# Matmul order in the FFN up projections of a two-layer trunk: both column halves of a strip per input block, high parts first and then low parts

## The reference

```python
D_MODEL = 1024
SEQ = 256
DEPTH = 2
FFN_HIDDEN = ((8 * D_MODEL + 3 * 256 - 1) // (3 * 256)) * 256      # 2816
...
    for i in range(DEPTH):
        ...
        mix = jnp.concatenate([prim, mo], axis=-1) @ w_out[i]
        h = h + rmsnorm(mix, post_mix_g[i])
        hn = rmsnorm(h, pre_ffn_g[i])
        gu = hn @ w_ffn_in[i]
        ff = (jax.nn.silu(gu[..., :FFN_HIDDEN]) * gu[..., FFN_HIDDEN:]) @ w_ffn_out[i]
        h = h + rmsnorm(ff, post_ffn_g[i])
    return h
```

## Time and profile before

| | |
|---|---|
| median of 3 runs | 777.34 us (775.53 to 777.49) |
| the profiled execution, its own time | 776.1 us |
| its span in the trace | 774.4 us |
| PE busy | 745.0 us, 96% of the span |
| DVE, ACT, POOL busy | 446.5, 393.7, 106.5 us |
| 640 matmuls of 512 columns in the wide strips (L1026) | 226.5 us busy |
| 640 matmuls of 256 columns in the wide strips (L1028) | 179.7 us busy |

### The profile page before, as it was taken

How to read it: one execution, slowest core, us unless ns; L and a number is a source line. 1 busy time by engine, 2 the same in 40 slices (tenths; PEclk the granted TensorE clock), 3 DMA queues, 4 the chain that set the end, 5 groups by cost and what they waited for, 6 DMA issues and landing times.

```text
span 774.4 us, 15179 instructions
## 1 busy us (share of the span) xinstructions
PE 745.0 (96%) x6549; PEld 639.3 (83%) x6549; DVE 446.5 (58%) x645; ACT 393.7 (51%) x654; POOL 106.5 (14%) x163
## 2 busy tenths in 40 slices
PE   5999999999999999999999999999899999999996
PEld 4789966678888888888888878999788888888885
DVE  4777886647766566432242638533657756756423
ACT  5835766548645455422465435523248545555311
POOL 8020076500000000000300056500000000000000
PEclk9999989999999999999999999999999999999999
DMA  9847700026655555464733330000055655655411
GB/s 311 301 142 234 251 31 2 2 84 222 203 170 194 187 174 207 166 209 154 237 112 115 120 136 20 4 5 4 3 168 187 195 186 178 202 167 206 172 54 55
DMA packets 78277, 111.71 MB, mean 144 GB/s; under 512 B 2124, under 2 KB 64738, under 8 KB 78210
## 3 DMA queue, kind: packets, MB, share of 16 engines
q1 hardware_dynamic: 77090, 107.67, 41.9%
q0 software_dynamic: 976, 3.04, 1.2%
q10 hardware_dynamic: 144, 0.04, 0.0%
HBM read 109.68 MB, written 1.05 MB: 143 GB/s over the span
## 4 chain that ended last, share of the span: by engine, by line
PE 89%; DVE 5%; ACT 3%; issue 1%; DMA 1%; POOL 0%; DVEq 0%; SPq 0%; ACTq 0%
PE ps L1026 19%; PE ps L726 11%; PE ps L1187 10%; PE ps L727 10%; PE ps L728 10%; PE ps L1028 10%; PE ps L1014 8%; PE ps L760 2%; PE ps L895 1%; PE ps L869 1%; PE ps L846 1%; DMA hn<-mem 1%; DVE row_max L1896 1%; ACT scores L1411 1%; DVE x_hi_lo L2046 1%
## 5 line engine op out<-in xcount | busy, mean ns | idle before, releaser
L1825 DVE TENSOR_TENSOR w_lo<-w_raw,w_hi 128x2048 fp32r<-128x2048 f32 (+2 forms) x90 | 202.2, 2260 | 83.7 <-ACT w_hi L1359 83.6
L1026 PE MATMUL ps<-x_hi_lo,w_hi 128*128 128x512 f32 x640 | 226.5, 399 | 0.0
L1359 ACT ACTIVATE w_hi<-w_raw 128x2048 fp32r<-128x2048 f32 (+2 forms) x90 | 168.0, 1886 | 38.9 <-PE ps L728 37.6
L1028 PE MATMUL ps<-x_hi_lo,w_lo 128*128 128x256 f32 x640 | 179.7, 281 | 0.0
L1026 PEld LDWEIGHTS ps<-x_hi_lo,w_hi 128*128 128x128 f32 x640 | 120.3, 188 | 29.8
L1028 PEld LDWEIGHTS ps<-x_hi_lo,w_lo 128*128 128x128 f32 x640 | 120.9, 189 | 0.0
L726 PE MATMUL ps<-w_hi,x_hi_lo 128*128 128x512 f32 (+3 forms) x208 | 74.1, 356 | 2.8 <-DVE x_hi_lo L2046 2.0
L727 PE MATMUL ps<-w_lo,x_hi_lo 128*128 128x512 f32 (+3 forms) x208 | 72.2, 347 | 0.0
L728 PE MATMUL ps<-w_hi,x_hi_lo 128*128 128x512 f32 (+3 forms) x208 | 72.1, 347 | 0.0
L726 PE MATMUL ps<-w_hi,hidden_hi 128*128 128x512 f32 x176 | 69.6, 395 | 0.0
L728 PE MATMUL ps<-w_hi,hidden_lo 128*128 128x512 f32 x176 | 69.5, 395 | 0.0
(11 more groups left out here) (365 smaller groups left out, 1012.5 us busy)
## 6 DMA issues: line engine op xcount, KB each, us to landing
w_raw<-w_ffn_in SPq DMA_DIRECT2D x44, 1024.0 KB, 5.0
w_raw<-w_ffn_out SPq DMA_DIRECT2D x22, 1024.0 KB, 5.0
w_raw<-rwkv_w_in SPq DMA_DIRECT2D x11, 1024.0 KB, 5.4
w_raw<-w_out SPq DMA_DIRECT2D x8, 1024.0 KB, 5.0
w_raw<-nsa_w_in SPq DMA_DIRECT2D x6, 1024.0 KB, 15.0
w_raw<-w_mem_kv SPq DMA_DIRECT2D x2, 1024.0 KB, 8.9
w_raw<-nsa_cmp_k_w SPq DMA_DIRECT2D x2, 1024.0 KB, 5.5
w_raw<-nsa_cmp_v_w SPq DMA_DIRECT2D x2, 1024.0 KB, 5.4
```

The lines of the kernel that those rows point to most:

```text
L1026: pe.matmul(psum[:, bank + j, :], kt_of(w_hi, i, k)[:, c], xx[:, k, :, :].rearrange("p c n -> p (c n)"), start=k == 0, stop=False)
L1028: ins = pe.matmul(psum[:, bank + j, 0:SEQ], kt_of(w_lo, i, k)[:, c], xh[:, k, :], start=False, stop=k == KD - 1)
L1359: act.activation(w_hi[:, i % SPL, 0:size(i)], raw[:, i % RAW, 0:size(i)], ACT.Copy).then_inc(hi_done, 1)
L1825: dve.tensor_tensor(w_lo[:, i % RAW, 0:size(i)], raw[:, i % RAW, 0:size(i)], w_hi[:, i % SPL, 0:size(i)], ALU.subtract).then_inc(lo_done, 1)
```

## The change

Inside `wide_strip` the loops change places. Before, half 0 went through all 8 input blocks, high and low matmul in turn, and then half 1. Now each input block is gone through once: the 512-column matmul of half 0, that of half 1, then the 256-column matmul of half 0, that of half 1. The operands, the sizes, the number of matmuls and of weight loads, the waits and the increment of `used` are the same.

```diff
             def wide_strip(i, bank):
 
                 pe.wait_ge(lo_done, split_no(i) + 1)
-                for j in range(2):
-                    c = slice(P * j, P * j + P)
-                    for k in range(KD):
-                        pe.matmul(psum[:, bank + j, :], kt_of(w_hi, i, k)[:, c], xx[:, k, :, :].rearrange("p c n -> p (c n)"),
+                cols = [slice(P * j, P * j + P) for j in range(2)]
+                for k in range(KD):
+                    for j in range(2):
+                        pe.matmul(psum[:, bank + j, :], kt_of(w_hi, i, k)[:, cols[j]], xx[:, k, :, :].rearrange("p c n -> p (c n)"),
                                   start=k == 0, stop=False)
-                        ins = pe.matmul(psum[:, bank + j, 0:SEQ], kt_of(w_lo, i, k)[:, c], xh[:, k, :],
+                    for j in range(2):
+                        ins = pe.matmul(psum[:, bank + j, 0:SEQ], kt_of(w_lo, i, k)[:, cols[j]], xh[:, k, :],
                                         start=False, stop=k == KD - 1)
                 ins.then_inc(used, 1)
```

## The result

The changed kernel takes 771.85 us (median of 4 runs, 770.31 to 773.02) beside 777.41 us for the kernel before in the same measurement (4 runs). The ratio is 0.9939, 95% interval 0.9918 to 0.996: it is faster, by 3.1 to 6.4 us. The forecast was no change, with 770.9 to 781.6 as the range and 16 in 100 for faster. Ratios leave out one of e4's ten runs, which took 1058.93 us at a mean granted clock of 0.656, where its other nine had 0.993 to 0.996; what lowered the clock there is not known.

The account below looks back on a forecast made before the run. The prediction took PE's own pace to bound the wide strips. Every term came to 0 us, leaving the profiled execution's 776.1 us, put at 777.3 to suit the runs' median; range 770.9 to 781.6.

Parts of the forecast that it names:

- rival 2: Wide strips: spare time between matmuls shrinks in the new order, −6.4 us to 770.9, or −4.3 us to 773.0; 16 in 100.
- What bounds the kernel: Wide strips: nothing but PE's own pace sets them; PE is busy for 745.0 of 774.4 us.
- Count of work, waits, consumers, weight loads: Wide strips: equal instruction counts, no added waits, consumers and slots released as before, loads hidden under matmuls; 0 us each.
- Rival 1: Second narrow slot of each group: a weight load shows, +22.4 us, or +2.3 to +4.3 in small form; 13 in 100.
- PSUM banks: Wide strips: changing bank costs nothing, and writing the second bank 2.8 us earlier adds no wait; 0 us.
- Rival 3: Wide strips: changing banks with every matmul makes PE wait and lowers its clock, +226.1 us to 1003; 1 in 100.
- Order of the matmuls: Groups of four in wide strips: spacings summed from other loops give 0.7067 us, as before the change; 0 us.

Follow-up runs that it names:

- e4: Changed kernel's order of widths and banks, but half 1 takes the input block beside half 0's, so no neighbours share a block; ratio 0.9963 to the kernel before.
- e2: Kernel before with widths still alternating, but 512-column matmuls of one half interleaved with 256-column ones of the other, changing bank behind nearly every matmul; ratio 1.0.
- e5: Kernel before with all 16 wide matmuls of a strip first, halves by turns, then the 16 narrow ones; ratio 0.9962.
- e3: Kernel before, still half 0 then half 1, but two input blocks at a time as 512, 512, 256, 256 to one bank; ratio 0.9956.
- e1: Kernel before with each input block gone through once, but widths alternating: 512 and 256 of half 0, then of half 1; ratio 1.0007.
- e10: Kernel before with the hidden tiles and the small tiles behind them moved up by 256 bytes in each partition; 777.15 us in one run.
- e12: Kernel before with input tile `x_hi_lo` and all that stands behind it moved up by 384 bytes in each partition, weights unmoved; ratio 0.9956.
- e9: Kernel before with the hidden tiles and the small tiles behind them moved up by 640 bytes in each partition; ratio 0.996.
- e7: Kernel before with only the last wide strip of each layer ordered 512, 512, 256, 256 to one bank; 774.8 us in one run.
- e8: Kernel before with one more PE wait ahead of each layer's down projection, until ACT has copied the last strip's results; ratio 1.0021.

## Why the prediction was wrong in its mechanism, and right in its range

The forecast was "same within 0.3%", and that did not come: the kernel is faster by more. The time of 771.85 us lies in the range all the same, 0.95 us above its lower end. That end was priced for rival 2, from the lowest spacings of two other loops, and neither loop's spacings are what the strips took; that it held is partly luck.

**What bounds the kernel.** Right. PE is busy for all of each stretch before and after, the clock stands at 1.00 in both, and PE waits for nobody in the strips.

**Count of work, waits, consumers, weight loads.** Right, at 0 us each. Loads in the second narrow slot are hidden; narrow pairs even got shorter. Rival 1 did not occur.

**PSUM banks.** Right at 0: e2 changes the bank behind nearly every matmul and keeps 5.653 us, ratio 1.0. Rival 3 did not occur: the granted clock is 1.00 in the strips of the changed kernel and of e2. The Trainium skill (TensorE: Matmul & The Clock Gate, A second HAM failure mode: psum-queue depth-cycling) tells of a kernel that cycles through PSUM banks, idles briefly between groups of matmuls and swings between the two clocks. These two traces change banks and show no such swing.

**Order of the matmuls.** This step failed: "a matmul's cost here goes by its own width and not by its neighbour's". I had priced the new order from pure runs, 2 × 0.2333 + 2 × 0.120 = 0.7067 us, and took it as proof that this was what the alternating group cost. It was a coincidence: two errors cancelled. In the alternating strips a wide matmul costs 0.2367 us, 0.0033 more than priced, and a narrow one 0.1167, 0.0033 less; the earlier trace rows already had 0.24 and 0.11 to 0.12 as single spacings. The 0.2333 was the down projection's own value at its own place in memory, and a run of 16 wide ones in the strips has 0.228 (e5). Nor are the mixed orders sums of pure ones: pairs cost 0.6967, alternation 0.7067. It is rival 2 that came, at half its price: 0.010 us a group in place of 0.0201, 3.2 us in place of 6.4. "Nothing in the trace ties it to the order" was true of that trace, and I read it as evidence against, though the out and the down projection with equal shapes and unequal spacings said plainly that my price list lacked a variable.

**What the cause is, and what stays open.** Shown: the change's gain comes with grouping equal widths. e3 has the grouping without the other two, e1 and e2 have the other two without it, and every trace with grouped widths has strips of 5.57 to 5.59 us in both layers. Alternating strips have 5.653 in every trace with the tiles at their old places and in e10; they have 5.618 in e12 and 5.546 in layer 1 of e9. So the order decides for the tiles as they lie, and not once for all. Shown too: the down projection's spacing depends on what ran ahead of it (e7, e8), and the spacing of a 512-column stream on where its operands lie (e9, e10, e12). Not shown: whether the width or the tile of the loads counts (above), and the mechanism below that. That a weight load and the streaming of the matmul before it get in each other's way would fit, but no run tests it. The Trainium skill (TensorE: Matmul & The Clock Gate, Step-by-step: what each phase is for) says that loading the next weights takes no read bandwidth from the running matmul. That gives no reason for e9's 0.0067 us a matmul after a move of 640 bytes; no run here shows what does.

**Size.** The four-run medians give −5.6 us, the two spans −3.1. Strips (3.16) and down projection (0.5) explain some 3.7 us; e3 and e4 measured 2.9 to 3.4. The rest of the 5.6 has no place in the trace, and the interval of 3.1 to 6.4 us takes in 3.7.

## What to carry to other kernels

- On a path that TensorE alone sets, spacings between matmul starts are to be read for the very sequence in question. A price from a run of one width, or from another loop with the same shapes, was off here by 0.003 us a matmul in the strips and by up to 0.0067 between two loops; that two such errors cancel in a sum proves nothing about its terms.
- Where wide and narrow matmuls alternate, try equal widths grouped by two beside the old order. Longer runs brought no more here (5.57 and 5.59 us against 5.57), and in one stretch (e9, layer 1) the old order was the faster one.
- If two loops with equal shapes have different spacings, compare the addresses of their stationary operands before looking for waits. Moving tiles by some hundred bytes gave as much (ratio 0.996) as reordering 1280 matmuls. Then look at every stretch: a move meant for one loop changed another here.

## What the runs showed of the hardware that I had not expected

With 512 columns of rounded float32 streamed and 128×128 loaded, starts are 0.2267 us apart or 0.2323 to 0.2334. With the weights, which are streamed, at multiples of 256 bytes from the arena's base, the stationary operand's place decides:

| stationary operand, kernel | bytes past a multiple of 256 | spacing, us |
|---|---|---|
| `x_hi_lo`, before | 0 | 0.2266 |
| `hidden_hi`, before / changed | 128 | 0.2333 / 0.2323 |
| `hidden_hi`, e10 | 128 | 0.2333 |
| `hidden_hi`, e9 | 0 | 0.2267 |
| `hidden_hi`, e12 | 0 | 0.2267 |
| `x_hi_lo`, e12 | 128 | 0.2334 |
| `mem_hi` and `mem_lo`, before | 128 | 0.2323 |
| `mem_hi` and `mem_lo`, e12 | 0 | 0.2268 |

The last two rows are of a projection near the kernel's start, whose stationary tiles begin where `hidden_hi` begins in the kernel before and moved by the 384 bytes of e12. No experiment aimed at it, which makes it an independent check. The 22 spacings are 26.92 − 21.81 = 5.11 us in the kernel before and 26.48 − 21.49 = 4.99 us in e12:

```profile
21.81 0.39 PE L727 MATMUL ps<-w_lo,mem_hi 128*128 128x512 f32 x1
...
26.92 0.40 PE L728 MATMUL ps<-w_hi,mem_lo 128*128 128x512 f32 x1
```

```profile
21.49 0.40 PE L728 MATMUL ps<-w_lo,mem_hi 128*128 128x512 f32 x1
...
26.48 0.39 PE L729 MATMUL ps<-w_hi,mem_lo 128*128 128x512 f32 x1
```

All placements go by the same line. The weights were never moved, so whether the distance between the two operands counts or the stationary one's address alone is open; the wide strips gained 0.035 us each when only their moving operand went from 0 to 128 (e12), so a rule "same place is good" does not hold for them in the alternating order.

In the slow placement the spacing also depends on how the stream was entered, and it then stays for the 264 matmuls: 0.2333 behind alternating strips, 0.2323 behind pairs (e7) or a stall (e8). The order ahead is not all that sets it. The `mem_hi` stream, with the same program ahead of it in both kernels, has 0.2323 in the kernel before and (27.47 − 22.34) / 22 = 0.2332 in e1.
